# A retention, attention and mixture network on one core: the projections of the retention's heads 1 to 7 read and write their 512 columns in runs out of order

## What is computed

```
def project(h):
    p = h @ w_in
    q = _heads(p[..., :RET_QK_W], RET_HEADS, RET_DK).astype(jnp.float32) * (RET_DK ** -0.5)
    k = _heads(p[..., RET_QK_W:2 * RET_QK_W], RET_HEADS, RET_DK).astype(jnp.float32)
    v = _heads(p[..., 2 * RET_QK_W:2 * RET_QK_W + RET_V_W], RET_HEADS, RET_DV).astype(jnp.float32)
    g = p[..., 2 * RET_QK_W + RET_V_W:]
    return q, k, v, g
...
q_c, k_c, v_c, g_c = project(h_ctx)
q_l, k_l, v_l, g_l = project(h_lat)
```

## Time and profile before

| | |
|---|---|
| device time, median of 2 executions | 3269.69 us (3269.02 to 3270.36) |
| span of the profiled execution, first to last instruction | 3265.3 us |
| median over the span (what lies around it) | 4.4 us |
| PE busy | 3195.3 us, 98% of the span |
| PEld, DVE, ACT busy | 2772.3, 1757.6, 1298.9 us |
| mean granted TensorE clock | 0.995 |

### The profile page before, as it was taken

The page is one execution under the profiler, slowest core; times in us unless marked ns, Lnnn a source line. Parts: engine busy times, 40 slices in busy tenths (PEclk is TensorE's granted clock), DMA queues, the critical chain, the costliest instruction groups (busy, mean ns, idle before and its releaser), DMA issues.

```text
span 3265.3 us, 48483 instructions
## 1 busy us (share of the span) xinstructions
PE 3195.3 (98%) x20556; PEld 2772.3 (85%) x20556; DVE 1757.6 (54%) x2600; ACT 1298.9 (40%) x1878; POOL 0.2 (0%) x4
## 2 busy tenths in 40 slices
PE   8999999999999999999998999999999999999998
PEld 6677777878778787777876889988999999999998
DVE  5543544444444444444446667778676665555555
ACT  4443222232322323222234645556554444444443
POOL 0000000000000000000000000000000000000000
PEclk9999999999999999999999999999999999999999
DMA  9854433233333333323334434445655545556564
GB/s 369 317 192 174 174 110 133 93 110 136 116 123 104 116 110 128 130 104 119 107 123 162 133 106 146 152 130 172 199 167 180 172 154 168 181 189 199 194 194 149
DMA packets 153928, 508.98 MB, mean 156 GB/s; under 512 B 15345, under 2 KB 35953, under 8 KB 152945
## 3 DMA queue, kind: packets, MB, share of 16 engines
q1 hardware_dynamic: 149328, 493.03, 44.4%
q10 hardware_dynamic: 4384, 12.85, 1.0%
HBM read 501.62 MB, written 4.19 MB: 155 GB/s over the span
## 4 chain that ended last, share of the span: by engine, by line
PE 90%; DVE 4%; ACT 2%; DMA 2%; issue 1%; SPq 1%; ACTq 0%; DVEq 0%
PE bank L590 28%; PE bank L592 27%; PE bank L591 27%; PE bank L652 3%; PE bank L835 1%; DMA raw<-stream 1%; DVE w_lo L1677 1%; PE bank L816 1%; ACT w_hi L1084 1%; PE bank L826 1%; SPq L563 0%; PE bank L668 0%; ACT a_s L1392 0%; DVE a_s L2084 0%; DMA raw_h<-stream 0%
## 5 line engine op out<-in xcount | busy, mean ns | idle before, releaser
L590 PE MATMUL bank<-h_hi,w_hi 128*128 128x256 f32 (+1 forms) x4032 | 1259.7, 312 | 10.7 <-DVE w_lo L1677 5.1
L592 PE MATMUL bank<-h_hi,w_lo 128*128 128x256 f32 (+1 forms) x4032 | 1239.8, 307 | 0.0
L591 PE MATMUL bank<-h_lo,w_hi 128*128 128x256 f32 (+1 forms) x4032 | 1239.1, 307 | 0.0
L1677 DVE TENSOR_TENSOR w_lo<-raw,w_hi 128x1024 fp32r<-128x1024 f32 x729 | 881.5, 1222 | 585.7 <-ACT w_hi L1084 581.3
L1084 ACT ACTIVATE w_hi<-raw 128x1024 fp32r<-128x1024 f32 x729 | 761.5, 1057 | 914.3 <-PE bank L592 568.7
L590 PEld LDWEIGHTS bank<-h_hi,w_hi 128*128 128x128 f32 x4032 | 759.3, 188 | 83.4 <-issue 39.2
L591 PEld LDWEIGHTS bank<-h_lo,w_hi 128*128 128x128 f32 x4032 | 759.6, 188 | 44.9 <-issue 3.1
L592 PEld LDWEIGHTS bank<-h_hi,w_lo 128*128 128x128 f32 x4032 | 759.1, 188 | 43.8
L590 PE MATMUL bank<-w_hi,h_hi 128*128 128x512 f32 x704 | 286.6, 407 | 12.5 <-DVE w_lo L1677 6.2
L592 PE MATMUL bank<-w_hi,h_lo 128*128 128x512 f32 x704 | 276.6, 393 | 0.0
L591 PE MATMUL bank<-w_lo,h_hi 128*128 128x512 f32 x704 | 275.9, 392 | 0.0
(11 more groups left out here) (257 smaller groups left out, 2890.4 us busy)
## 6 DMA issues: line engine op xcount, KB each, us to landing
raw<-stream SPq DMA_DIRECT2D x904, 512.0 KB, 4.2
raw_h<-stream SPq DMA_DIRECT2D x32, 512.0 KB, 10.0
res<-tokens_in ACTq DMA_DIRECT2D x4, 1024.0 KB, 8.8
vg<-mem_in ACTq DMA_DIRECT2D x4, 512.0 KB, 8.7
h_hi<-mem_kv ACTq DMA_DIRECT2D x2, 1024.0 KB, 9.7
out<-res SPq DMA_DIRECT2D x4, 512.0 KB, 3.0
mem_kv<-qk ACTq DMA_DIRECT2D x1, 1024.0 KB, 7.9
mem_kv<-vg ACTq DMA_DIRECT2D x1, 1024.0 KB, 7.5
```

The costliest lines, as they stand in the source:

```text
L590: pe.matmul(out, sh, mh, start=start, stop=False, **checks)
L591: pe.matmul(out, sh, ml, start=False, stop=False, **checks)
L592: return pe.matmul(out, sl, mh, start=False, stop=stop, **checks)
L1677: dve.tensor_tensor(in_quarters(m.low(raw)[:, :]), m.raw[SLOT[raw]], in_quarters(m.w_hi[slot][:, :]).bitcast(F32), ALU.subtract).then_inc( ...
```

## The change

The list `RUNS` gives each retention head an order for the 512 columns of its `qk` and `g` tiles: head 0 keeps the plain order, and heads 1 to 7 have a run length n and a flag `far`. `ordered` rearranges the view of the operand, and `tile` applies it to the moved operand (`h_hi`, `h_lo`) and to the bank alike, so that product column c still lands in column c of the bank. Nothing in memory is laid out anew.

- `far` true, heads 1 to 4, n = 2, 4, 8, 16: n columns of the first half (latents), the n columns with the same place in the second half (context, 256 columns further), the next n of the first half, and so on. Runs in a matmul: 256, 128, 64, 32.
- `far` false, heads 5 to 7, n = 4, 8, 16: every second run of n over all 512 columns, then the runs between them. Runs in a matmul: 128, 64, 32.

```
+RUNS = [None, (2, True), (4, True), (8, True), (16, True), (4, False), (8, False), (16, False)]
...
+    def ordered(x, runs):
+
+        if runs is None:
+            return x
+        n, far = runs
+        return x.rearrange("p (m o i) -> p o m i", m=2, i=n) if far else x.rearrange("p (o m i) -> p m o i", m=2, i=n)
+
     def tile(what, cols, k_tiles=KT, k0=0, acts=None, between=None):
 
         xh, xl = acts or ((m.h_hi, m.h_lo) if what[0] in ("qk", "g") else (m.h2_hi, m.h2_lo))
-        out = bank(*what)[:, 0:cols.stop - cols.start]
+        runs = RUNS[what[1]] if what[0] in ("qk", "g") else None
+        out = ordered(bank(*what)[:, 0:cols.stop - cols.start], runs)
...
-                mm = product(out, (wh[:, w], wl[:, w]), (xh[:, k0 + k, cols], xl[:, k0 + k, cols]),
+                mm = product(out, (wh[:, w], wl[:, w]),
+                             (ordered(xh[:, k0 + k, cols], runs), ordered(xl[:, k0 + k, cols], runs)),
                              k == 0, k == k_tiles - 1)
```

## The result

The changed kernel takes 3335.27 us (median of 3333.36 and 3337.18) against 3269.69 us: the ratio is 1.0202, with a 95% interval of 1.0184 to 1.022, so 65.6 us slower. That the change is slower is clear; whether by more or less than 2% the two executions leave open. The profiled execution's span is 3335.9 us against 3265.3, +70.6 us. Its device time is 3337.18 us, so 1.3 us lie around a span; the prediction's 4.4 us compared two different executions.

The account below looks back on a forecast made before the run. PE's rate of moving columns was taken to set the end, uncovered, in the changed heads. Four costs of 0 left the span of 3265.3 us, and with 4.4 us around it 3270 us, range 3262 to 3362 us.

Parts of the forecast that it names:

- the prediction's 4.4 us: Time around the profiled execution's span, added to the span of 3265.3 us to give the forecast.
- rival B: Operand supply limited by groups of four words: only head 1's runs of 2 slow, to twice; +87.0 us, 3357 us; chance 0.13.
- C: Each new run costs a tick: 3389 us, or 3347 us if already paid once in 16 columns; chance 0.10, half each.
- A: Main case for the changed matmuls: nothing measurable, 3270 us, own range 3262 to 3280; chance 0.61.
- part 2: Reading the moved operand in runs in the changed matmuls: taken as 0, between 0 and 609 us.
- Part 3: Writing the bank in the same runs: same bounds and one cost with the reading, taken as 0.
- Part 1: Decoding the longer access form of 2688 matmuls: 0.112 us of slack for each pair, taken as 0.
- Part 4: Readers of the banks (L1874, L1745, L1149), in plain order from a bank filled at the same time: 0.
- D: Any order that is not plain halves the flow in all seven heads alike: +609 us, 3879 us; chance 0.10.
- E: Plain order causes the 32 extra ticks a matmul and the other orders don't: -35.8 us, 3234 us; chance 0.02.

Follow-up runs that it names:

- e5: Changed kernel with the bank written plainly and the moved operand read in 64 orders, one a tile (shifts, streams by turns, repeated words); 3376.82 us.
- e2: Changed kernel with the moved operand read plainly and only the bank written in the seven orders; 3269.06 us, beside 3268.14 us for the kernel before.
- e4: Changed kernel with the bank written plainly and the operand read in runs of n every s columns, another pair in each tile; 3557.51 us.
- w1: Kernel before, with split products of 512 columns reading two streams by turns, bank written plainly and read with a step of 2; 3190.02 us, 0.9761.
- e7: Changed kernel with q, k and gate products from bfloat16 constants, operand read in 37 orders, one a tile, bank written plainly; 3450.82 us.

## Why the prediction was right or wrong

The reading of the kernel was right: PE sets the end in these heads, nothing covers a slower matmul, no instruction moved, and the matmuls of the seven heads give 69.3 us of the 71.5 us that PE is busy longer. The forecast value, 3270 us for no cost at all, was wrong. Its range, 3262 to 3362 us, held the result only because it was drawn over rival B and the lower price of C, which had 0.18 of the chances together; that the time lies between A and them is no merit of A's mechanism.

**The step that failed is part 2, the reading of the moved operand,** taken at 0 between 0 and 609 us "by the pair of L1754 and L1757". It costs some 69 us. The choice went by rows of another engine, and by the more convenient two of three: L1757 and L1790 are both a TENSOR_SCALAR, L1754 is another operation with two tensors read, and L1790 against L1757 said 54% more for pairs. And the better evidence stood in the same text: 544 ticks for 512 columns, an excess that had no explanation. e5 shows what kind it was: the plain row is already bound by how its words are fetched (226.7 ns, against 215.8 where each column is read twice in a row or two streams take turns), so there was no slack in which a worse order could hide.

**Part 3, the writing,** was taken at 0 and is 0 (e2). **Part 1,** the longer form, is 0: six forms with two more dimensions ran at 215.8 ns in e5. **Part 4** is 0 as far as the totals tell: DVE is busy 1758.4 us for 1757.6 and ACT 1300.6 for 1298.9.

**Rival B** had the mechanism: groups of four words at the limit of their supply. It put head 1 at +87 us and the others at 0; head 1 is +41 and the others +26.9. So its total is near by two errors that offset each other in part. Its doubling is what runs of 2 cost up to a step of 128 (431 to 487 ns in e4) but not at 256, head 1's own, with 333 ns. That a line which is soon come back to is cheaper would explain this; no run isolates it. Nor does any explain why runs of 4 to 16, which use every line whole, cost 2 to 10% more than the plain row. **Rival C** gave 3347 us by a tick for each run beyond one in 16, the nearest figure and not a mechanism: head 1 has 256 extra ticks for its 256 runs and head 4 has 32 for its 32, but head 2 has 56 for 128 and head 5 about 10 for 128. **D** is out. **E**, that the plain order causes the 32 ticks, had a chance of 0.02 and was half right: none of the seven orders gains, but others do, and w1 makes use of it.

**The two rules cited.** The Trainium skill, "Advanced Engine Details and Errata", section PSUM Cachelines, says "Any non-contiguous AP significantly slows down matmuls" (AP is the access pattern). That doesn't hold for these writes: e2 writes in runs of 2 to 16, near and far, at 70.29 us a window. The Trainium skill, "SBUF — State Buffer", section Door 1, wants at least two hits on a 16-byte line for full bandwidth. It has the line right (e5: runs of 4 moved by 4 take 231 ns, moved by 1 to 3 at least 453) and the count wrong here: two hits give half the rate in float32 and in bfloat16 (453 ns), four give 226.7 ns in the plain float32 row, and 215.8 ns takes eight in the plain bfloat16 row, or two streams by turns in float32.

## What to carry to other kernels

Look at the distance of starts of the moved operand's matmuls before anything else: 512 columns of split float32 take 226.7 ns in the plain order, and 215.8 ns is the least that any order took here. At 226.7 ns, read two stretches by turns (column c of each half after the other), write the bank plainly and let its readers on DVE and ACT take it by a step of 2, which costs them nothing (691, 688 and 597 ns as before): 2.4% here from the products of 512 columns. Don't cut the moved float32 operand so that a 16-byte line gives fewer than four columns a visit (431 ns and more at most steps), and begin runs on a line; even runs of 4 and more cost up to 22% by the step (e4). The order in which the bank is written was free for the seven orders of e2, at 226.7 ns a matmul. In bfloat16 leave the plain order as it is.

## What the hardware showed that was not expected

- A visit of a 16-byte line costs about 1.77 ns in both types at small steps, also where the granted clock is at half. Windows of PE in e7, (1, 8) early and late in its tile, clock 0.50, and (1, 4), clock 1.00:

```profile
314.80:317.50 2.70, 2.70 (x5) 0.50 0.85 306
340.00:345.00 5.00, 5.00 (x7) 0.50 0.00 0
289.40:292.00 2.60, 2.60 (x7) 1.00 0.01 3
```

  (1, 8) has 512 visits in 0.90 us (1.76 ns each) at 1.2 GHz and (1, 4) 256 visits in 0.452 us (1.77 ns each) at 2.4 GHz. So the time of a visit doesn't follow the granted clock.
- The start of a plain row matters by up to 5%: 226.7 ns where the kernel has it, 229 to 238 ns moved by 1 to 32 columns, also by 4, 8, 16 and 32, which are whole lines (232 to 233). Why the place matters was not tried.
- Jumps between lines cost something even in runs of 16 and 32 (233 to 240 ns), and the same order takes 220 or 231 ns in different tiles. No rule for this was found.
- The gain by turns is one of the split float32 type alone: in bfloat16 two streams by turns take 486 ns for the plain 215.8. That even and odd places have a path each in the one type and share one in the other fits most orders, is argued from times, and leaves lines that are come back to unexplained in both (333 for 453 ns in float32, 486 for 907 ns in bfloat16).
